# Two attention stages of a fused transformer program: query tiles multiplied in two halves, and a reordered start of the last attention

## The reference

```
# sparse attention: queries, keys, values, then three softmax branches
proj = h @ w_in
q = rope(rmsnorm(q)); k = rope(rmsnorm(k))
hid = gelu(blocks @ cmp_w1 + cmp_b1)          # compressed keys and values
comp = hid @ cmp_w2
o = g0 * attend(q, k_cmp) + g1 * attend(q, k_slc) + g2 * attend(q, k_win)

# the last attention: 16 query heads share 4 key heads
q = rope(hn @ w_q) * head_dim ** -0.5
m = max(max(mask(q @ k)), sink)
p = exp(s - m) / (sum(exp(s - m)) + exp(sink - m))
o = p @ v
out = o @ w_out
```

## Time and profile before

| what | value |
|---|---|
| median of three runs | 1766.34 us |
| lowest and highest of them | 1762.69 us, 1768.07 us |
| the profiled execution's own time | 1767.22 us |
| its span in the trace | 1765.5 us |
| TensorE, VectorE, ScalarE busy | 97%, 68%, 51% of the span |
| mean granted clock of TensorE | 0.985 |

### The profile page before, as it was taken

One profiled execution on the slowest core, in us unless ns is written; L12 is line 12 of the kernel. 1 busy time (PEld: TensorE's weight loads), 2 busy tenths in 40 slices (PEclk: granted clock), 3 DMA queues, 4 the chain that ended last, 5 costly groups with the idle time before them and its releaser, 6 DMA issues.

```text
span 1765.5 us, 33377 instructions
## 1 busy us (share of the span) xinstructions
PE 1719.8 (97%) x13738; PEld 1622.4 (92%) x13738; DVE 1206.4 (68%) x1988; ACT 906.5 (51%) x1548; POOL 127.8 (7%) x165
## 2 busy tenths in 40 slices
PE   8999999999899999999999999999999998999998
PEld 7889998897699989999988799999999997699998
DVE  6887876667786767666555468664677657777664
ACT  7665455436764455444455445444554545555442
POOL 4110501100010001000000020000000010010000
PEclk8999999999999999999999999999999999999999
DMA  5335656431055555555533225555455552145553
GB/s 190 108 105 190 220 183 208 159 120 37 15 189 185 188 202 193 176 172 182 191 117 120 96 96 191 176 171 194 142 185 184 191 203 93 50 158 191 182 200 120
DMA packets 77048, 276.88 MB, mean 157 GB/s; under 512 B 8737, under 2 KB 10401, under 8 KB 76769
## 3 DMA queue, kind: packets, MB, share of 16 engines
q1 hardware_dynamic: 76320, 272.15, 46.0%
q0 software_dynamic: 288, 2.30, 0.4%
q10 hardware_dynamic: 288, 0.30, 0.0%
HBM read 273.66 MB, written 1.05 MB: 156 GB/s over the span
## 4 chain that ended last, share of the span: by engine, by line
PE 90%; DVE 6%; ACT 2%; issue 1%; DMA 1%; DVEq 0%; ACTq 0%
PE acc L2032 47%; PE mix L2032 19%; PE acc L2028 6%; PE acc L2029 3%; PE acc L2052 2%; PE mix L355 1%; DVE wl L2330 1%; PE mix L2137 1%; DVE x L2375 1%; PE mix L912 1%; PE mix L2052 1%; DMA arrived<-in_w 1%; DVE y L2369 1%; PE acc L2137 1%; ACT xh L2203 1%
## 5 line engine op out<-in xcount | busy, mean ns | idle before, releaser
L2330 DVE TENSOR_TENSOR wl<-arrived,wh 128x1024 fp32r<-128x1024 f32 x514 | 643.0, 1251 | 368.1 <-ACT wh L2190 355.4
L2190 ACT ACTIVATE wh<-arrived 128x1024 fp32r<-128x1024 f32 x514 | 541.1, 1058 | 572.1 <-DMA arrived<-in_w 571.3
L2032 PE MATMUL acc<-xh,wh 128*128 128x256 f32 (+1 forms) x1504 | 431.9, 287 | 3.5 <-DVE wl L2330 3.4
L2032 PE MATMUL acc<-xh,wl 128*128 128x256 f32 (+1 forms) x1504 | 427.9, 285 | 0.0
L2032 PE MATMUL acc<-xl,wh 128*128 128x256 f32 (+1 forms) x1504 | 426.7, 284 | 0.0
L2032 PE MATMUL acc<-hx,wh 128*128 128x256 f32 (+1 forms) x1664 | 302.9, 283 | 0.0
L2032 PEld LDWEIGHTS acc<-xh,wh 128*128 128x128 f32 x1504 | 285.5, 190 | 9.1 <-DVE wl L2330 4.4
L2032 PEld LDWEIGHTS acc<-xl,wh 128*128 128x128 f32 x1504 | 285.7, 190 | 0.2
L2032 PEld LDWEIGHTS acc<-xh,wl 128*128 128x128 f32 x1504 | 285.4, 190 | 0.0
L2032 PE MATMUL mix<-xh,wh 128*128 128x256 f32 (+1 forms) x960 | 273.8, 285 | 0.9 <-DVE wl L2330 0.9
L2032 PE MATMUL mix<-xh,wl 128*128 128x256 f32 (+1 forms) x960 | 272.3, 284 | 0.0
(11 more groups left out here) (473 smaller groups left out, 2142.2 us busy)
## 6 DMA issues: line engine op xcount, KB each, us to landing
arrived<-in_w SPq DMA_DIRECT2D x514, 512.0 KB, 3.3
scr<-in_cmp_w POOLq DMA_DIRECT2D x1, 2048.0 KB, 8.7
out<-x SPq DMA_DIRECT2D x8, 128.0 KB, 1.7
x<-in_x SPq DMA_DIRECT2D x3, 272.0 KB, 5.4
scr<-in_par SPq DMA_DIRECT2D x4, 123.0 KB, 6.5
x<-in_x ACTq DMA_DIRECT2D x1, 272.0 KB, 4.5
par<-in_par SPq DMA_DIRECT2D x1, 235.0 KB, 8.0
scr<-in_positions POOLq DMA_DIRECT2D x1, 128.0 KB, 3.6
```

Source lines behind the costliest of these rows:

```text
L2032: ins = nc.tensor.matmul(bank(name, t)[:, 0:L - c], w_part[:, h.slot, w], v_part[:, k, c:], start=(k == 0 and w_part is wh and v_part is h ...
L2190: nc.scalar.activation(wh[:, h.slot, :], raw(h.slot), ACT.Copy).then_inc(w_hi, 1)
L2330: nc.vector.tensor_tensor(wl[:, h.slot, :], raw(h.slot), wh[:, h.slot, :].bitcast(F32), ALU.subtract).then_inc(w_lo, 1)
```

## The change

In the sparse attention each query tile's eight blocks are multiplied in two halves of four (`some=range(0, 4)` and `range(4, KD)`). `compress`, `gates`, `place` and `values` move from behind a tile into the gap between the halves of a later tile; `compress` runs in two blocks of eight steps instead of 5, 5 and 6. The order of the small products among each other, and VectorE's and ScalarE's streams, are the same in that stage.

In the last attention, `normal(0)` goes ahead of `least(2)` and `least(3)` on VectorE, rotation 3 goes ahead of the loop, and `perm(3)` and `turned(0)` go ahead of `scores(2)` on TensorE. Seven products that nothing reads (`unread`, into the bank `stat`) stand between the first steps. One split moves ahead of the norm's root and its inverse on ScalarE and VectorE; VectorE's others move to later places, the last two into pairs 6 and 7; ScalarE's third goes behind `exps(0)` and `exps(1)`.

```diff
-        KEY_PARTS = {2: (0, 5), 3: (5, 10), 4: (10, 16)}
+        KEY_PARTS = {3: (0, 8), 4: (8, 16)}
...
             for m in range(KD):
-                gemm("nsa_q", xh, xl, META, None, first=m, last=m + 1)
+                gemm("nsa_q", xh, xl, META, None, first=m, last=m + 1, some=range(0, 4))
+                if m in KEY_PARTS:
+                    pe.wait_ge(n_used, SMALL.index(("r", 1)) + 1)
+                    compress(0, *KEY_PARTS[m])
+                if m == 2:
+                    small("gates", 0)
+                elif m == 4:
+                    small("place", 0)
+                elif m in (6, 7):
+                    small("values", m - 6)
+                gemm("nsa_q", xh, xl, META, None, first=m, last=m + 1, some=range(4, KD))
...
-                if m in KEY_PARTS:
-                    pe.wait_ge(n_used, SMALL.index(("r", 1)) + 1)
-                    compress(0, *KEY_PARTS[m])
-                if m == 1:
-                    small("gates", 0)
-                elif m == 3:
-                    small("place", 0)
-                elif m in (5, 6):
-                    small("values", m - 5)
...
+            def unread(n):
+                for _ in range(n):
+                    nc.tensor.matmul(stat[:, 0:SEQ], ones[:], cosT[:, 0:SEQ], start=True, stop=True)
+
             perm(0)
             perm(1)
+            pe.wait_ge(root_ok, norm_of(8) + 1)
+            unread(2)
             pe.wait_ge(acc_used, TILE["swa_q"] + 3)
             pe.wait_ge(s_kk, 2)
             scores(0)
             perm(2)
+            unread(1)
             scores(1)
-            pe.wait_ge(root_ok, norm_of(8) + 1)
+            pe.wait_ge(acc_used, TILE["swa_q"] + 4)
+            perm(3)
+            unread(4)
             for p in range(KD + 1):
                 if p:
                     values(p - 1)
+                else:
+                    turned(0)
                 if p + 2 < KD:
                     scores(p + 2)
-                if p + 3 < KD:
+                if p and p + 3 < KD:
                     perm(p + 3)
-                if p < KD:
+                if p and p < KD:
                     turned(p)
...
             nc.scalar.activation(sqrt_set[:], eps[:, 0:1], ACT.Exp)
-            for m in range(3):
-                ahead(BASE["swa_q"] + m)
+            ahead(BASE["swa_q"] + 1)
...
             exps(0)
             exps(1)
+            ahead(BASE["swa_q"] + 2)
...
             rotated(1)
-            ahead(BASE["swa_q"])
             dve.wait_ge(s_nk, 1)
             dve.wait_ge(s_mask, 3)
             least(0)
             least(1)
             sines(2)
             rotated(2)
-            ahead(BASE["swa_q"] + 1)
+            normal(0)
             least(2)
             least(3)
-            ahead(BASE["swa_q"] + 2)
+            sines(3)
+            rotated(3)
             for p in range(KD):
...
-                normal(p)
-                if t < KD:
+                if p:
+                    normal(p)
+                if 3 < t < KD:
                     sines(t)
...
                 if p >= 2:
                     attn_lo(dve, p - 2, 3)
+                if p >= 6:
+                    ahead(BASE["swa_q"] + p)
                 dve.wait_ge(s_pm, p + 1)
...
-                if t < KD:
-                    ahead(BASE["swa_q"] + t)
+                if p < 5:
+                    ahead(BASE["swa_q"] + p + 1)
...
             for u in range(0, upto):
+                if u == 8:
+                    ahead(BASE["swa_q"])
                 rooted(norm_of(u), c0(u))
...
             for u in range(0, upto):
+                if u == 8:
+                    ahead(BASE["swa_q"])
                 rms(norm_of(u), c0(u), rx)
```

More of the change, by code:

```diff
@@ L2015, in _, with half @@
             pe.wait_ge(const_ok, 7)
-            def half(h, name, t, part, hi, lo, c, kt, wait):
-                pe.wait_ge(w_lo, h.n + 1)
-                if part == 0:
+            def half(h, name, t, part, hi, lo, c, kt, wait, some=None):
+                ks = range(part * KD, min(kt, part * KD + KD)) if some is None else some
+                if ks[0] % KD == 0:
+                    pe.wait_ge(w_lo, h.n + 1)
+                if ks[0] == 0:
                     bank_free(pe, name, t)
-                ks = range(part * KD, min(kt, part * KD + KD))
                 for k in ks:
@@ L2034, in half, with gemm @@
                                                stop=(k == kt - 1 and w_part is wl))
-                ins.then_inc(used, 1)
-            def gemm(name, hi, lo, c, wait, kt=KD, first=0, last=None):
+                if ks[-1] == min(kt, part * KD + KD) - 1:
+                    ins.then_inc(used, 1)
+            def gemm(name, hi, lo, c, wait, kt=KD, first=0, last=None, some=None):
                 parts = -(-kt // KD)
@@ L2043, in gemm @@
                         half(Half(BASE[name] + t * parts + part), name, t, part, hi, lo, c, kt,
-                             wait if t == 0 else None)
+                             wait if t == 0 else None, some)
             def opening(group, hi, lo, c, hi_ok, lo_ok, norm=None):
```

## The result

| | before | after |
|---|---|---|
| median of five runs | 1763.35 us | 1753.99 us |
| lowest and highest | 1761.92 us, 1768.07 us | 1753.00 us, 1757.91 us |
| span of the profiled execution | 1765.5 us | 1756.2 us |
| mean granted clock in it | 0.985 | 0.990 |

The ratio is 0.9949 with a 95% interval of 0.9927 to 0.9971: 0.5% faster, by about 9 us. The forecast was 1762.0 us, most likely within 0.3%, with a range down to 1758.5. The measured median lies 4.5 us under that range. The forecast was wrong, although, as the rows now show, each move in the last attention came out within 0.1 us of it.

The account below looks back on a forecast made before the run. TensorE, busy 97% of the span, was taken to bound the kernel. Terms -4.2 - 1.5 + 0.8 = -4.9 us on 1767.22 us gave 1762.3, taken as 1762 us, range 1758.5 to 1766.8.

Parts of the forecast that it names:

- The last attention, -4.2 us: Start of the last attention: query tile 4 starts 4.2 us earlier, 1.5 us from the clock, the rest from the order.
- The sparse attention, -1.5 + 0.8 us: Sparse attention's query tiles: 1.5 us regained from tile 4 at half clock, 0.8 us added by five more interruptions.
- C: Experiments' theory: stages before the change lose more half clock on average than the profiled execution showed; sparse attention -3 us or more.
- Rival 1: Clock fall moves to last attention's query tile 4 or sparse query tiles' end; 1763.8 or 1765.3 us; chance 0.23 with rival 3.
- the rule on transposes: Transposes don't hold the full clock as products do; it could fall over `turned(0)` and halve query tile 4: 1763.8 us.
- Rival 2: Last attention: clock falls ahead of the four unread products, which run at 1.2 GHz; slower, 1768.5 us; chance 0.09.
- Rival 3: Sparse part returns nothing: clock falls elsewhere there or the fall was that execution's own; 1763.8 us; chance 0.23 with rival 1.
- Rival 4: More saved: clock holds in later stages too, or measured executions held more half clock; 1.5 to 3 us, 1759.5 us; chance 0.18.
- A: Experiments' theory: the change gives what its own stages show, some 5 us; clock falls elsewhere differ from execution to execution.

Follow-up runs that it names:

- e2: The kernel before with only the last attention's hunks and the split moved ahead of the root; 1759.15 us, ratio 0.9969.
- e3: The changed kernel once more, unaltered, compared with the kernel before; 1756.49 us, ratio 0.9961.
- e7: The changed kernel with `gates`, `place` and `values` back behind their tiles, only `compress` between halves; 1756.22 us, ratio 0.9960.
- e10: The changed kernel with `gates`, `place` and `values` back behind tiles and VectorE's last three splits one place later; 1756.28 us, ratio 0.9962.
- e9: The kernel before once more, unaltered, measured as if it were a change; 1761.09 us, ratio 0.9984.
- e5: The kernel before with twelve unread products in the last attention's three starting waits, its order otherwise kept; 1760.73 us, ratio 0.9991.
- e11: The changed kernel with `normal(0)` behind `least(2)` and `least(3)` on VectorE again; 1756.81 us, ratio 0.9960.
- e12: The changed kernel with eight unread products instead of the last four, in front of `turned(0)`; 1757.6 us in its one run.
- e6: The kernel before with all 16 steps of `compress` in one block behind query tile 4; 1763.57 us, ratio 1.0008.

## Why the prediction was wrong

**The last attention, -4.2 us: right, in size and in each step.** Counted from the first `scores`, predicted and measured: `scores(1)` 3.18 and 3.19 us; `normal(0)` done 6.1 and 6.2; `turned(0)` 6.3 and 6.35; `scores(2)` 7.8 and 7.86; query tile 4 8.7 and 8.77. VectorE waited 0.52 us for the exponentials (0.6 predicted), the late splits left 0.26 us of their covers (0.25), and the four unread products ended 0.16 us behind `normal(0)` (0.2). All traces with this start unaltered (e2, e3, e7, e10 and after) keep 41.8 us from the first to the last `scores`, so the shift was carried. Of the two things that hold it up, the order, with the moved splits, is the larger (2.9 us) and the clock the smaller (1.0 to 1.4); the forecast had 2.7 and 1.5.

**The sparse attention, -1.5 + 0.8 us: right in kind, both sizes off.** The interruptions cost 78.3 - 77.9 = 0.4 us against the old order without a fall (e9), not 0.8. What was saved wasn't the one fall of 1.5 us: the old order had no fall in e9 (77.9 us), one in the trace of before and in e5 (79.4 both), and two in e2 (80.9). The new order had none in eight traces (78.2 to 78.4 us). So the part gives between +0.4 and -2.6 us by execution, about -1.1 where the old order has one fall; forecast -0.7. The four traces of the old order have one fall on the mean, as the profiled execution has, so C finds no support here.

**The rivals.** Rival 1 fell at the places that it named: with order and unread products together the clock was 1.00 from `scores(0)` through query tile 4 in all seven traces, and the sparse query tiles had no fall. There the rule on transposes in the Trainium skill, "TensorE: Matmul & The Clock Gate", section "Part 4: PE-mode transpose", doesn't show: the six transposes of `turned(0)` ran their 0.82 us at the full clock, and tile 4 behind them too. The falls of e11 and e12 in the last pairs say that the earlier trace rows doesn't hold in every trace; which of `scores`, transposes or the waits between them is behind it stays open. Rival 2 fell with rival 1. Rival 3 is true of some executions, as e9 shows. Rival 4 forecast the time that came nearest, but its reasons aren't borne out: the 93 runs of before hold less of the half clock than the profiled execution (what the clock withheld is worked out below: 22.7 us on the mean, against 26.5 in the profiled one), and the linear attention, a later stage, doesn't gain on the mean (585.4 us with the change ahead of it and without).

**The step that failed is the base.** The forecast put -4.9 us on "the profiled execution's 1767.22 us" and took 1762. That execution, and the median 1766.34 of the three runs, lie high: 93 later runs of the same kernel have a median of 1762.38 us, in sets of 1762.19, 1761.62 and 1763.20. The traces show it in place, where the code is the same in all 13: the profiled execution of before took 330.2 us up to the sparse attention's first small product (mean of the other twelve 328.5, highest 330.0) and 587.8 us in the linear attention (585.2; only e11 took longer), 4.4 us more than the mean. The same sum on 1762.38 is 1757.5, and with -5.3 us from the rows (-4.2 in the last attention, -1.1 in the sparse attention) 1757.1, already under the 1758.5 at which the range ends; twelve runs of the changed kernel gave 1756.49. The range was built from unknown costs of the change and let the base move by 1 us, though the three runs shown spread over 5.4 and the later ones over 16. The first five runs of the changed kernel, 1753.99, were on the low side as well (1756.49 in the twelve). So of the 8.0 us from the forecast down to 1753.99 the base is 4.5 (1762 to 1757.5), the size of the sparse term 0.4, and 3.1 no row explains; 2.5 of these are the difference between the five runs and the twelve.

**Why the base moves.** Each run lists its span and clock, and span x (1 - clock) is what the clock withheld. Over the 93 runs of before this is 12 to 34 us with a mean of 22.7, and it goes with the time at a correlation of 0.88, 0.84 us of time for 1 us. This supports A, and the linear attention shows it in place: 582.3 to 591.6 us in 13 traces, the lowest and the highest both in versions of the changed kernel.

**What stays open.** The 17 runs of the changed kernel (five and twelve) have a mean of 14.9 us withheld, 7.8 less than before. One fall of 3.4 us at half clock in the sparse attention and one of 6.8 in the last attention account for 1.7 + 3.4 = 5.1 of that; two falls and the 10.2 us of e9 would account for more. Whether the last 2 to 3 us are that, or chance, the traces don't settle. In time, rows give -5.3 us and the measured medians -5.9 (1762.38 to 1756.49) to -9.4 (the first five of each). The ratios of e3, e7, e10 and e11, 0.9960 to 0.9962, stand for -6.7 to -7.0 us of 1762.38, and all four intervals hold -5.3. With e9 at 0.9984 for no change at all, the first two don't differ measurably. To fix where the falls land was not tried, since no edit here controls it.

## What to carry to other kernels

Put a worked-out saving on a median of many runs, not on the profiled execution: a kernel whose clock falls at varying places has a base that moves more than the change is worth, and the range must hold that movement. A stream written anew from durations of the trace can be right to 0.1 us where one engine's waits end on another's; reorder first, since products that only hold the clock gave 1.0 us where the order gave 2.9, and count a filler as free only as long as its end is covered: four too many cost 1.7 us. A half-clock stretch in one trace is a sample: look at several before pricing its removal.

## What the runs showed of the hardware that was not expected

- The same work in the same order, in programs that differ at most in other stages: falls of the clock in the sparse query tiles none, one or two (77.9, 79.4, 80.9 us), and up to 9 us between linear attentions (582.3 to 591.6 us).
- Half clock cost almost nothing where TensorE waited for VectorE: e9 had 10.2 us of it in the start of the last attention where before had 6.8, and lost 0.3 us.
- Interrupting a query tile for other products costs little: 0.4 us for five interruptions; tile 4 took 3.13 us in two halves for 2.93 in one.
- All 16 steps of `compress` in one block (e6) brought one fall, not more than three short blocks; all five falls seen in the query tiles began at the end of such a block or less than 1 us behind it.
- The last pairs, at 1.00 in eleven traces, had a fall in e11 and e12: `values` took 41.0 and 40.9 us from first to last, for 39.9.
